# Eight of 63 selection steps of the sample group moved from a prompt tile to the latent stage

## What is computed

```python
def block(args):
    qa, qi, wi, pb = args
    dots = jnp.einsum('bqhd,bkd->bqhk', qi, k_idx, preferred_element_type=jnp.float32)
    score = jnp.einsum('bqh,bqhk->bqk', wi.astype(jnp.float32), jax.nn.relu(dots))
    score = jnp.where(key_pos <= pb[..., None], score, -jnp.inf)
    _, sel = lax.top_k(score, top_k)
    ...
```

## Time and profile before

| | |
|---|---|
| median of 3 runs | 3501.96 us (3500.55 to 3503.51) |
| the profiled execution | 3497.13 us, of which its span 3495.4 us |
| TensorE matmuls busy | 3000.5 us, 86% |
| TensorE weight loads busy | 2573.4 us, 74% |
| VectorE busy | 1468.3 us, 42% |
| ScalarE busy | 969.0 us, 28% |
| GpSimd busy | 620.7 us, 18% |
| mean granted TensorE clock | 0.922 of 2.4 GHz |
| ("D", 0) tile | 751.65 to 768.89 us in the first layer |
| latent stage, first value matmuls of pairs 0, 1, 2 | 969.19, 1003.03, 1034.48 us in the first layer |

### The profile page before, as it was taken

One profiled execution on the slowest core, in us unless ns is written; L12 is line 12 of the kernel. 1 busy time (PEld: TensorE's weight loads), 2 busy tenths in 40 slices (PEclk: granted clock), 3 DMA queues, 4 the chain that ended last, 5 costly groups with the idle time before them and its releaser, 6 DMA issues. The chain is left out here.

```text
span 3495.4 us, 46062 instructions
## 1 busy us (share of the span) xinstructions
PE 3000.5 (86%) x18298; PEld 2573.4 (74%) x18298; DVE 1468.3 (42%) x2158; ACT 969.0 (28%) x1542; POOL 620.7 (18%) x562
## 2 busy tenths in 40 slices
PE   6999978768786779999989999786687868799997
PEld 6999758545564669998689997684555656699985
DVE  2222353477664352222622224434876633422236
ACT  2222222434332221222322223224343222222223
POOL 1111020113112131110211111102121121411103
PEclk9999989879898789999989999897898989899998
DMA  3222431300121232224432234313001223222244
GB/s 110 81 78 90 145 118 44 121 1 1 61 79 74 97 87 82 78 79 131 127 92 78 78 109 140 103 34 121 1 1 61 92 89 100 72 82 80 79 138 129
DMA packets 241755, 293.95 MB, mean 84 GB/s; under 512 B 12625, under 2 KB 205489, under 8 KB 235457
## 3 DMA queue, kind: packets, MB, share of 16 engines
q1 hardware_dynamic: 234688, 229.00, 21.7%
q0 software_dynamic: 6912, 62.92, 4.8%
HBM read 287.72 MB, written 3.88 MB: 83 GB/s over the span
## 5 line engine op out<-in xcount | busy, mean ns | idle before, releaser
L132 DVE TENSOR_TENSOR wlo<-raw,whi 128x1024 fp32r<-128x1024 f32 (+1 forms) x412 | 537.1, 1304 | 1455.7 <-ACT whi L128 1454.5
L128 ACT ACTIVATE whi<-raw 128x1024 fp32r<-128x1024 f32 (+1 forms) x412 | 433.5, 1052 | 1601.8 <-PE ps L467 929.1
L467 PE MATMUL ps<-xth,whi 128*128 128x296 f32 x2816 | 811.1, 300 | 43.7 <-DVE wlo L132 43.7
L467 PE MATMUL ps<-xtl,whi 128*128 128x296 f32 x2816 | 813.2, 301 | 0.0
L467 PE MATMUL ps<-xth,wlo 128*128 128x296 f32 x2816 | 615.6, 300 | 0.0
L467 PEld LDWEIGHTS ps<-xth,whi 128*128 128x128 f32 x2816 | 533.8, 190 | 44.6 <-DVE wlo L132 44.6
L467 PEld LDWEIGHTS ps<-xtl,whi 128*128 128x128 f32 x2816 | 532.5, 189 | 0.0
L467 PEld LDWEIGHTS ps<-xth,wlo 128*128 128x128 f32 x2816 | 461.0, 189 | 0.0
L140 PE MATMUL ps<-whi,hth 128*128 128x512 f32 (+1 forms) x880 | 350.5, 398 | 10.0 <-DVE wlo L132 8.3
L142 PE MATMUL ps<-whi,htl 128*128 128x512 f32 (+1 forms) x880 | 346.9, 394 | 0.0
L141 PE MATMUL ps<-wlo,hth 128*128 128x512 f32 (+1 forms) x880 | 346.8, 394 | 0.0
(11 more groups left out here) (372 smaller groups left out, 4021.2 us busy)
## 6 DMA issues: line engine op xcount, KB each, us to landing
raw<-in_ffn_w_in SPq DMA_DIRECT2D x176, 512.0 KB, 3.8
raw<-in_ffn_w_out SPq DMA_DIRECT2D x176, 512.0 KB, 3.5
raw<-in_w_o SPq DMA_DIRECT2D x32, 512.0 KB, 3.6
raw<-in_w_in SPq DMA_DIRECT2D x16, 507.0 KB, 3.8
gb<-in_ln_g SPq DMA_DIRECT2D x6, 512.0 KB, 4.5
gb<-in_ln_b SPq DMA_DIRECT2D x6, 512.0 KB, 5.9
raw<-in_w_in SPq DMA_DIRECT2D x8, 338.0 KB, 3.6
x<-in_x_prompt SPq DMA_DIRECT2D x1, 1536.0 KB, 11.0
```

The costliest lines, as they stand in the source:

```text
L128: e.activation(T.whi[:, s % SPLIT, 0:width], T.raw[:, s, 0:width], ACT.Copy).then_inc(S.hi_done, 1)
L132: e.tensor_tensor(T.wlo[:, s % SPLIT, 0:width], T.raw[:, s, 0:width], T.whi[:, s % SPLIT, 0:width].bitcast(F32), ALU.subtract).then_inc(S. ...
L467: mm = e.matmul(bank(u, up)[:, h, :], part[:, s, w], xp[:, k, o], start=(k == 0 and part is T.whi and xp is T.xth), stop=(k == KD - 1 and ...
```

## The change

`("D", 0)` leaves `STEP_UNITS`, so that the prompt stage issues 24 steps instead of 32, beginning in D1. The latent stage issues 39 instead of 31: the steps ahead of the copies of transposed probabilities are five instead of three in each of pairs 0, 1 and 2, which makes 13 places per pair, all of them used. Which value each step computes is unchanged.

```diff
-STEP_UNITS = [("D", 0), ("D", 1), ("D", 2), ("D", 3)]
+STEP_UNITS = [("D", 1), ("D", 2), ("D", 3)]
 STEPS_HERE = 8 * len(STEP_UNITS)
 STEPS_THERE = 2 * TOPK_S // 8 - STEPS_HERE
...
                 for ch in early(p):
                     chunk_out(ch)
                 if M and p < PAIRS - 1:
-                    steps(3)
+                    steps(5)
                 if p > 0 and not M:
                     mix_out(e, p - 1)
                 for g in range(5):
```

## The result

The changed kernel takes 3523.3 us (median of 7 runs, 3511.73 to 3526.87); the kernel before took 3500.55 us beside it (7 runs, 3495.21 to 3504.44). The ratio is 1.0061, with a 95% interval of 1.0046 to 1.0076: 16 to 27 us slower, 21 us by the ratio. The forecast was 25 us, 3527 us in a range of 3517 to 3533.

What follows compares the result with a forecast made beforehand. TensorE, 86% busy, was taken as the bound, VectorE steps costing only where TensorE waits behind them. Tile -0.3, steps ahead of the copy +20.5, clock +5.1 gave +25.3 us: 3501.96 + 25 = 3527 us, range 3517 to 3533.

Steps and rivals of the forecast that it cites:

- The tile: Diagonal prompt tile: heads stay 1.42 us apart without the eight steps; only 0.15 us a layer gained at its edge.
- Rival 4: Diagonal tile: VectorE paces it, so it shrinks by 2.6 us in both layers, still ending at 3525 us; chance 0.04.
- The steps ahead of the copy: Latent pairs 0 to 2: added steps delay the copy TensorE needs by 2.59, 2.59, 5.05 us; 20.5 us in both layers.
- rival 3: Latent stage: added steps are covered because TensorE's wait has another cause than the copy; 3502 us, chance 0.04.
- The clock: Latent value matmuls: TensorE's clock falls after waits; 2.2 us a layer in pair 2, 0.7 us in second-layer pair 0; 5.1 us.
- Rival 1: Latent pair 2: the low clock does not come, or comes shorter; 20 us slower, 3522 us, chance 0.18.
- Rival 2: Latent stage: longer waits lengthen the low clock in all six pairs; 28 us slower, 3530 us, chance 0.20.

Runs made afterwards that it cites:

- experiment 1: Kernel before, with the diagonal tile's eight steps moved to the very start of the latent stage; 3498.22 us, ratio 1.0004 to before.
- experiment 8: Kernel before, with two steps instead of one in each head of the diagonal tile and 23 in the latent stage; 3512.7 us, ratio 1.0042.
- experiment 2: Kernel before, with each pair's three steps behind the copy of the first transposed probabilities instead of ahead of it; 3481.64 us, ratio 0.9957.
- experiment 4: Changed kernel, with each pair's five steps behind copies (three behind group 0's, two behind group 2's); 3483.48 us, ratio 0.9957 to before.
- experiment 6: Changed kernel, with all eight added steps in pair 0, eleven ahead of its first copy; 3516.79 us, ratio 1.0046 to before.
- experiment 7: Changed kernel, with all eight added steps in pair 2, nine ahead of its first copy; 3525.42 us, ratio 1.0079 to before.
- experiment 5: Kernel before, with the tile's eight steps at the latent stage's start and each pair's three behind group 0's copy; 3481.4 us, ratio 0.9947.

## Why the prediction was right

**The tile.** The step was right and a little small: 0.28 us a layer where I took 0.15 us. The handover at the tile's edge gave 0.15 us, as read; most of the rest is a head in the middle (the reduction at 763.23 in the kernel before, 0.37 us after its L1413 at 762.86) that a match-replace had held up by 0.11 us. My sum did not have it. That VectorE's being nearly full did not make it the pacer is shown from both sides, by experiment 1 (a step less, 1.42 us) and experiment 8 (a step more, 2.67 us). Rival 4 is out.

**The steps ahead of the copy.** Forecast 2.59, 2.59 and 5.05 us; measured 2.59, 2.59 and 5.07 us in the first layer, 2.61, 2.60 and 5.07 us in the second (by the idle time ahead of L2016 in pair 0, from the start of the second group of transposes to L2016 in the others). 20.5 us forecast, 20.5 us found. Experiments 2 and 4 show the mechanism by its removal, and rival 3 (cover) is out.

**The clock.** The mechanism was right, the size 1 us too large in the sum: 5.1 us forecast. The six stretches from L2016 to L1970 are 9.24, 9.74 and 10.26 us, then 9.36, 9.98 and 10.39 us, which is 12.2 us above 7.79 us each, against 8.1 us before: 4.1 us more. Pair 2 paid 2.5 and 2.6 us, more than my 2.2 us; pair 0 of the first layer paid 1.45 us and not 2.13 us, and the second layer's pair 0 stayed at 1.6 us, where I had expected 2.2 us. The price in one pair is not a constant of the wait but scatters: 1.45 to 2.6 us here, up to 2.8 us in experiment 7 (10.58 us from L2016 to L1970 after a wait of 3.17 us). So that the sum of six came within 1 us is partly luck: the two pairs 2 paid 5.1 us where I had 4.4 us, and the other four paid 1.0 us less than before where I had 0.7 us more. The Trainium skill (page "TensorE: Matmul & The Clock Gate", section "HAM oscillation — how this bites in real kernels") takes half of the time at the low clock as lost. For the first layer's pair 2 that gives an estimate of 2.7 us, half of about 5.4 us (from 1043.5 on, PEclk 0.51 until 1049); the trace has 2.5 us, so it roughly agrees. Rival 1 (no low clock in pair 2) is out. Rival 2 (longer in all six with longer waits) is out by experiment 6: 13.58 us of wait, 9.77 us of stretch.

**The whole.** -0.56 + 20.5 + 4.1 = 24.0 us is accounted for by these terms. The stretches give 24.6 us with the tile; the 0.6 us between the two lies in the chunks between the pairs, where TensorE waits once for a chunk that ScalarE copies out (L1947 behind L2133): 1.15 and 0.74 us instead of 0.49 and 0.54 us in the first layer, 0.74 and 0.76 us instead of 0.85 and 0.94 us in the second. No term of my sum had it, and why these waits differ is open. Pair 3 adds 0.4 us more. The ratio of times, 16 to 27 us, contains all of these sums and does not tell them apart. The two profiled executions differ by more, 3526.87 against 3497.13 us: 5 us of that arise in the second layer's sparse stage, where the granted clock from 2894 to 2914 and to 2934 is 0.79 and 0.78, and at the same place in the kernel before, from 2870 to 2890 and to 2910, 0.91 and 1.00. Nothing of the change is there.

## What to carry to other kernels

Filler work on an engine is free or costly by what stands behind it in that engine's queue: ahead of a copy that TensorE waits for, each step cost its whole 1.3 us, behind the same copy nothing. An engine that looks 93% busy need not be the pacer; the test is the handover from the producer's start to its reader's start, compared with one place where the reader was idle. And a new wait of TensorE is to be charged twice, for its length and for the low clock behind it, here 1.45 to 2.8 us after each of the waits of 2.40 to 13.58 us ahead of the value matmuls that was left empty.

## What was not expected

TensorE's clock fell to 0.5 without a wait worth the name: in experiment 2, first layer, pair 1, after gaps of 0.83 us at most, in which TensorE was busy 0.40 to 0.63 of each microsecond from 993 to 996, and in pair 2 likewise. The same instructions with the same gaps in the second layer, and in experiments 4 and 5, kept 1.0. Pair 2 with one step ahead of its copy, on the other hand, kept its 1.58 us in both layers of the kernel before and of experiments 1 and 6, six times of six, and with five or nine steps there it took 2.88 us in both layers of the changed kernel and of experiment 7, four times of four; so the new low clock in pair 2 is the change's and not chance. Still, the clock's part of a difference as small as this has to be taken from several pairs, and a single profile can be over 1 us off in each.
